# Mixer 1: three modulation units move from TensorE to VectorE, and the places at which units are loaded and finished move

## What is computed

```python
c_act = jax.nn.silu(c)                                  # (1, 2048)
mod = (c_act @ w_ada[l] + b_ada[l])[:, None, :]         # w_ada is 2048 x 12288
sh1, sc1, g1, sh2, sc2, g2 = jnp.split(mod, 6, axis=-1)
h = rms_norm(x, norm_mix[l]) * (1.0 + sc1) + sh1
x = x + g1 * hybrid_mixer(h, w_in[l], w_out[l], ...)
...
proj = h @ w_in                                         # all heads from one projection
ret_out = retention_chunkwise(rq, rk, rv) ...           # 4 heads
rwkv_out = rwkv7_time_mix(...)                          # 8 heads, low-rank codes, a scan
moba_out = moba_attention(mq, mk, mv)                   # 8 heads, softmax
return jnp.concatenate([ret_out, rwkv_out, moba_out], axis=-1) @ w_out
```

## Time and profile before

| | us |
|---|---|
| median of 3 runs | 2505.76 |
| lowest, highest | 2505.07, 2507.09 |
| the profiled execution, its own time | 2505.68 |
| its span, first to last instruction | 2503.9 |
| PE busy | 2454.4 (98%) |
| DVE busy | 1543.8 (62%) |
| POOL busy | 1234.3 (49%) |
| ACT busy | 1130.6 (45%) |
| mean granted TensorE clock | 0.992 |

### The profile page before, as it was taken

How to read it: one execution, slowest core, us unless ns; L and a number is a source line. 1 busy time by engine, 2 the same in 40 slices (tenths; PEclk the granted TensorE clock), 3 DMA queues, 4 the chain that set the end, 5 groups by cost and what they waited for, 6 DMA issues and landing times.

```text
span 2503.9 us, 49446 instructions
## 1 busy us (share of the span) xinstructions
PE 2454.4 (98%) x19158; PEld 2258.4 (90%) x19158; DVE 1543.8 (62%) x2630; ACT 1130.6 (45%) x1351; POOL 1234.3 (49%) x502
## 2 busy tenths in 40 slices
PE   6999999999999999999999989999999999999998
PEld 5797998999999999998887968899999999998886
DVE  3537667666767777776666787366756756443333
ACT  2253334534444444454545444444444444454544
POOL 2674445775444444444444756575444444444443
PEclk9999999999999999999999989999999999999999
DMA  9974565796777777777776656476565575556553
GB/s 393 396 270 180 201 226 224 262 360 235 280 275 276 266 268 283 260 266 269 281 263 243 238 187 242 171 293 251 219 243 216 216 260 184 181 179 199 192 192 127
DMA packets 140524, 611.63 MB, mean 244 GB/s; under 512 B 15600, under 2 KB 15984, under 8 KB 115824
## 3 DMA queue, kind: packets, MB, share of 16 engines
q1 hardware_dynamic: 140112, 609.09, 66.8%
q10 hardware_dynamic: 288, 0.79, 0.1%
HBM read 607.72 MB, written 2.10 MB: 244 GB/s over the span
## 4 chain that ended last, share of the span: by engine, by line
issue 68%; POOL 30%; POOLq 1%; DMA 1%; ACT 0%
POOL wlo L1816 30%; DMA raw<-wstream 1%; POOLq L1813 1%; POOLq L1815 0%; POOLq L396 0%; ACT whi L1832 0%; POOL xT L1823 0%; POOLq L1816 0%; ACT hi_h L1832 0%; POOLq L3009 0%
## 5 line engine op out<-in xcount | busy, mean ns | idle before, releaser
L1816 POOL TENSOR_TENSOR wlo<-raw,whi 128x1024 fp32r<-128x1024 f32 x496 | 1230.6, 2486 | 1247.1 <-ACT whi L1832 1246.4
L1832 ACT ACTIVATE whi<-raw 128x1024 fp32r<-128x1024 f32 x760 | 800.8, 1059 | 923.9 <-PE psum L2059 775.1
L2059 PE MATMUL psum<-hi_h,whi 128*128 128x256 f32 x4224 | 1207.6, 286 | 5.5 <-DVE lo_h L2483 3.4
L2059 PE MATMUL psum<-hi_h,wlo 128*128 128x256 f32 x4224 | 1191.1, 282 | 0.0
L2059 PE MATMUL psum<-lo_h,whi 128*128 128x256 f32 x4224 | 1190.7, 282 | 0.0
L2059 PEld LDWEIGHTS psum<-hi_h,whi 128*128 128x128 f32 x4224 | 799.4, 189 | 19.6 <-issue 8.1
L2059 PEld LDWEIGHTS psum<-hi_h,wlo 128*128 128x128 f32 x4224 | 799.6, 189 | 1.5 <-issue 1.2
L2059 PEld LDWEIGHTS psum<-lo_h,whi 128*128 128x128 f32 x4224 | 799.2, 189 | 0.0
L2483 DVE TENSOR_TENSOR wlo<-raw,whi 128x1024 fp32r<-128x1024 f32 x264 | 388.1, 1474 | 280.2 <-ACT whi L1832 280.2
L2491 DVE SCALAR_TENSOR_TENSOR psum<-ada_raw,cact,psum 128x256 f32<-128x256 f32 x996 | 431.6, 485 | 28.3 <-DMA ada_raw<-adastream 18.1
L2059 PE MATMUL psum<-whi,gshi 128*128 128x512 f32 x704 | 276.4, 393 | 0.3 <-DVE wlo L2483 0.3
(11 more groups left out here) (175 smaller groups left out, 1585.1 us busy)
## 6 DMA issues: line engine op xcount, KB each, us to landing
raw<-wstream SPq DMA_DIRECT2D x760, 512.0 KB, 4.4
ada_raw<-adastream SPq DMA_DIRECT2D x168, 1024.0 KB, 6.7
arena<-adastream SPq DMA_DIRECT2D x24, 1024.0 KB, 18.1
xT<-x_in SPq DMA_DIRECT2D x8, 512.0 KB, 7.2
gs_pages<-tabs_in SPq DMA_DIRECT2D x2, 512.0 KB, 4.3
gs_pages<-rw_in SPq DMA_DIRECT2D x2, 512.0 KB, 7.0
y_out<-xT SPq DMA_DIRECT2D x2, 512.0 KB, 3.2
y_out<-xT ACTq DMA_DIRECT2D x1, 512.0 KB, 2.7
```

Source lines behind the costliest of these rows:

```text
L1816: nc.gpsimd.tensor_tensor(wlo[:, q, :], raw[:, q, :], whi[:, q, :].bitcast(F32), ALU.subtract).then_inc(sem.lo_ready, 1)
L1832: return nc.scalar.activation(out_, in_, ACT.Copy, scale=scale)
L2059: return nc.tensor.matmul(o, lhsT, rhs, start=start, stop=stop, skip_group_check=True)
```

## The change

- Units 16, 17 and 29 are made by DVE; only 18 and 28 remain with PE. `LATE_UNITS1` starts one unit earlier.
- DVE makes units 16 and 17 ahead of the token shift of the fourth group, and units 29 to 32 at the stage's end, with the second attention round between the 7th and 8th product of unit 31.
- PE finishes unit 16 after slab 28, inside `G_LORA`; unit 29 after slab 91; unit 30 after slab 95; unit 31 after slab 100. The spots at slabs 36, 88 and before `moba_scores(1)` are gone.
- SP's loads move: unit 17's from slabs 36 and 37 to 32 and 34, unit 30's from 88 and 89 to 94 and 96, unit 31's from 96 and 97 to 98 and 100, unit 32's from 100 and 101 to 103, both.

```diff
-SPOTS1 = (32, 36, 40, 44, 48, 52, 56, 60, 64, 68, 72, 76, 80, 84, 92, 96, 104)
+SPOTS1 = (28, 36, 40, 44, 48, 52, 56, 60, 64, 68, 72, 76, 80, 90, 94, 99, 104)
...
-LATE_UNITS1 = (START_UNITS + 14, MIX_UNITS1[1])
+LATE_UNITS1 = (START_UNITS + 13, MIX_UNITS1[1])
...
 def by_pe(u):
-    return u < LOOP_UNITS[0] or LOOP_UNITS[1] <= u < LATE_UNITS1[0]
+    return u < START_UNITS or u == LOOP_UNITS[0] - 1 or LOOP_UNITS[1] <= u < LATE_UNITS1[0]
...
-        first = spots[u - units[0] - 1] + 4 if u > units[0] else spot - 6
+        first = spots[u - units[0] - 1] + 4 if u > units[0] else spot - 2
...
-        gap = 2 if late else 3 if u == LOOP_UNITS[1] else 1
+        gap = 2 if late or u in (START_UNITS + 1, LATE_UNITS1[0] + 1, LATE_UNITS1[0] + 2) else 3 if u == LOOP_UNITS[1] else 1
+        gap = 0 if u == MIX_UNITS1[1] - 1 else gap
...
             group(G_LORA, 0, 4)
-            group(G_LORA, 4, 8)
+            group(G_LORA, 4, 5)
             spot()
+            group(G_LORA, 5, 8)
...
             group(G_TQK, 2, 4)
-            spot()
             pe.wait_ge(sem.lora_out, 1)
...
             moba_values(0)
-            fill(4)
+            fill(12)
             spot()
+
             fill(8)
             spot()
-
-            fill(10)
+            fill(2)
+            moba_scores(1)
+            fill(8)
             spot()
-            moba_scores(1)
-            fill(10)
+            fill(2)
             moba_turn(1)
...
                 if e == 3:
-                    unit_rows()
+                    loop_products(-3, 0, 16)
+                    loop_products(-2, 0, 16)
                 dve.wait_ge(sem.rw_self, e + 1)
...
+            loop_products(10, 0, 16)
             loop_products(11, 0, 16)
-            loop_products(12, 0, 16)
+            loop_products(12, 0, 7)
             dve.wait_ge(sem.mo_out, 1)
             moba_bias(1)
-            loop_products(13, 0, 10)
+            loop_products(12, 7, 16)
             moba_norm(1)
-            loop_products(13, 10, 16)
+            loop_products(13, 0, 16)
```

More of the change, by code:

```diff
@@ L2461, in _ @@
                 slab(n, pair_of(g), hhi[:, 2 * i:2 * i + 2, :], hlo[:, 2 * i:2 * i + 2, :], i == 0, i == GS - 1)
-            st.update(unit=MIX_UNITS1[0], units=MIX_UNITS1, spots=SPOTS1, slabs=3 * GS, after_taken={MIX_UNITS1[0]: 8})
+            st.update(unit=MIX_UNITS1[0] + 1, units=MIX_UNITS1, spots=SPOTS1, slabs=3 * GS, after_taken={})
             pe_mix1(pe, st, mm, part, spot)
```

## The result

| | before | with the change |
|---|---|---|
| median of 17 runs each, us | 2505.07 | 2510.21 |
| lowest, highest | 2503.11, 2507.09 | 2507.20, 2512.97 |
| the profiled execution, its own time | 2505.68 | 2507.36 |
| its span | 2503.9 | 2505.5 |
| mean granted clock of that execution | 0.992 | 0.991 |

The ratio is 1.0019, 95% interval 1.0013 to 1.0026: slower by 3.3 to 6.5 us. The forecast was 2501.6, between 2499.6 and 2504.3. The profiled execution with the change is one of the fastest of its 17, and is 1.68 us above the one before. So about a third of the loss can be read from the two traces; the rest has to come from the comparisons of runs.

The account below looks back on a forecast made before the run. PE, busy 98% of the span, was taken as the bound. From the profiled 2505.68 us, 3.8 in the low-rank chain and 0.3 at the stage's end were subtracted, giving 2501.6 us, range 2499.6 to 2504.3.

Parts of the forecast that it names:

- What goes from PE: Units 16, 17 and 29 leave PE's list: 2.03, 1.83 and 1.83 us, together 5.69; finishing of units costs the same.
- The units' cover at the fourth group: Units 16 and 17 fit into DVE's 21.38 us wait before the fourth group's token shift and cost nothing.
- the signs listed as wrong: DVE waiting for `ada_raw` in unit 17, no wait before the shift, `wlo` above 2.5 us, or no gap in `moba_turn(1)`.
- ACT and DVE have to be free for it; DVE was idle for some us ahead of each of its steps there: Low-rank chain: its steps follow PE's second product, 3.86 us earlier, so the scan begins 3.8 us earlier.
- the low-rank chain keeps one unit's gain: Rival: ACT's or DVE's work sets the chain, so 3.8 us becomes about 2.0; 2503.4 us, chance 0.13.
- What runs beside POOL: DVE's unit products beside POOL's `wlo` (2.40 us, under a slab's 2.88 on PE) would cost POOL nothing that shows.
- The stage's end, the wait: `moba_turn(1)`: slab 103 queues behind unit 32's load, PE waits 1.3 us, and 0.3 us of unit 29's gain is left.
- load plus slab: 6.1 us: Stage's end: slab 103, issued at 479.6 behind unit 32's load, lands 6.1 us after that load's issue, at 485.4.
- SP's wait starves the ring: Rival: unit 32's second half delays slabs 103 to 107; with unit 31's loads late, near 2511 us; chance 0.06.

Follow-up runs that it names:

- e5: e3 with ACT's rounding of slabs 40 to 42 made later, and POOL's `wlo` of them with it; 2500.05 us, ratio 0.9977 to the kernel before.
- e8: e1 with ACT's rounding of slabs 40 to 42 made later; 2500.44 us, ratio 0.9980 to the kernel before.
- e9: e3 with only POOL waiting: its `wlo` of slab 40 held until DVE's column work is done; 2501.79 us, ratio 0.9982 to the kernel before.
- e7: The kernel before with only ACT's rounding of slabs 40 to 42 made later, no unit moved; 2504.61 us, ratio 0.9994 to the kernel before.
- e2: The kernel before with only the change's late part (unit 29 by DVE, the stage's end and its loads); 2506.09 us, ratio 1.0004.
- e4: The kernel before with SP holding slab 103 until the second round's exponentials are made, no unit moved; 2507.91 us, ratio 1.0013.
- e1: The change without its late part: only units 16 and 17 moved to DVE; 2504.51 us, ratio 0.9999 to the kernel before.
- e3: The change with the load of unit 32's second half ahead of slab 105 instead of 103; 2505.03 us, ratio 0.9998 to the kernel before.
- e6: The change with only ACT's rounding of slabs 40 to 42 made later, unit 32's loads as in the change; 2505.45 us, ratio 0.9999 to the kernel before.

## Why the prediction was wrong

**What goes from PE: right.** 96 records, three units; finishing costs what it did.

**The units' cover at the fourth group: right.** Unit 16 ran 144.24 to 152.65 (forecast 143.96 to 152.4), unit 17 155.88 to 164.30 (155.5 to 163.9), the shift began at 166.14 (165.8) behind a wait of 1.85 (1.9). The second low-rank product came at 177.59 (near 177.2). None of the signs listed as wrong showed there: POOL's `wlo` beside the products took 2.40.

**"ACT and DVE have to be free for it; DVE was idle for some us ahead of each of its steps there": this step failed.** The transposes ahead of the scan began 0.96 us earlier, not 3.8 (1.3, if the 0.35 by which this execution was behind at 142 is added). DVE had one idle time of 3.02 us in the chain's second half, ahead of 184.73, and three steps behind it with no idle at all. I moved the chain by 3.8 us as a block and did not ask what stands beside it. POOL does not move with DVE: it follows ACT's `whi`. Where before the two TENSOR_TENSOR fell into a gap of POOL's, they now fell on two `wlo` and cost 4.2 us more; the scan cost 2.1 more, the steps with `mu` 2.0 more, and the last column steps, which had met POOL before, 4.4 less. That is 3.9 us more; less the row copy that is gone (0.41) and 0.23 at the first step, 3.3. DVE's steps began 1.24 us earlier (173.63 against 174.87), the 3.02 of idle went into them, and 0.96 was left at their end. e5, e8 and e9 take away the collisions behind 187, and PE's early stretch is 4.9 to 5.5 us shorter than before. That holds the column steps' old collision too; against e7, which is before without it, e8 is 3.9 us shorter (62.40 to 58.48), the gain of the two units in full.

The rival with this place, "the low-rank chain keeps one unit's gain", had the right engine ("ACT's or DVE's work") and came nearer (2.0 us kept; 1.0 to 1.3 were), but had no reason for it that names POOL. Its price of 2503.4 still counted a gain at the stage's end.

**What runs beside POOL: tried on the wrong instructions.** The rows: TENSOR_TENSOR on two operands in SBUF, 1.24 us each alone (2.48 for two) and 3.34 beside a `wlo`; four TENSOR_SCALAR in SBUF 1.14 alone, 5.50 beside; the products, whose second large operand is in PSUM, 0.53 a piece beside POOL, and POOL 2.40 beside them. The Trainium skill says in "SBUF — State Buffer", "Who interferes with whom", that a VectorE instruction with two SBUF inputs contends with a GpSimd instruction that reads SBUF, and that `tensor_scalar` can do so in its two-port modes. The trace agrees with the first by 3.34 against 1.24; the TENSOR_SCALAR here contended too, at 5.50 against 1.14, and whether they ran in such a mode no run shows. The prediction quoted the first half, tried it on the unit products, found nothing, and left the chain's own TENSOR_TENSOR out. Its "blocks" is one side only: the scan and the `wlo` each took longer where they came second, as the last section has it.

**The stage's end, the wait: mechanism right, size wrong.** PE entered `moba_turn(1)` 1.46 us ahead of where the early part alone would have put it (forecast 1.63; `moba_turn(0)` waited 0.39 us for ACT where 0.2 was priced), and SP's list held slab 103 behind unit 32's second half. The term that was mis-sized is "load plus slab: 6.1 us", taken from one row of before. Here slab 103 could be rounded 7.1 us after the load's issue (478.77 to 485.86), in e2 6.2; the load was issued 0.5 us later than its forecast. The wait was 2.59 where 1.3 was expected, and in e2, 1.32.

**No term for the clock: this step was missing.** The sum had PE's waits at their length. In the profiled execution the late wait cost 1.3 us beyond it (15.31 less 11.41, less 2.59; 1.07 of it behind `moba_turn(1)`), in e4, where it stands alone, 1.6 (15.27 less 11.41, less 2.28). This, and the wait's 1.3 us over forecast, are most of why the stage's end lost 2.4 us where 0.3 was to be gained (0.96 ahead at the transposes, 1.48 behind at slab 104).

Sum in the profiled execution: forecast -4.08 against its own time, measured +1.68. Of the 5.76 between them the chain has 2.8, PE's stay in `moba_turn(1)` 1.6 (4.26 us where 2.7 was forecast, 1.3 of it the longer wait), the clock behind it 1.1; 0.3 is left.

**What stays open.** The median is 3 us further up than the profiled execution shows. Over the 17 runs with the change the mean granted clock averages 0.9900, over the runs of before 0.9915 to 0.9918, and the runs at 0.989 took 2511.3 to 2513.0, those at 0.991 and 0.992 2507.2 to 2508.9. So the other executions lost more clock than the profiled one; where, no trace shows. The place ahead of the bonus sums is likely, as the change has a wait of 2.82 us there, and e1 and e3, with the same wait, had the low clock behind it. The means over the runs point the same way: 0.9911 with the early wait alone (e3, its runs of before 0.9918), 0.9907 with the late one alone (e6, its runs of before 0.9915), 0.9900 with both. That is argued, not shown. Low clocks also come and go where nothing was edited (560 to 620 us: 0.97 before, 1.00 with the change, each in its profiled execution).

Why the two halves, at 0.9999 and 1.0004 alone, come to 1.0019 together is another matter. e3 has both parts and the early wait and stands at 0.9998, so what is lost in addition goes with the late load: in e2 its wait was 1.32 us and lengthened PE's stretch by 1.3, in the change 2.59 and by 3.9.

The rival "SP's wait starves the ring" had the right queue and the right side, with 9.6 us from unit 31's loads; those came in time, and unit 31 ended at 478.74, not near 489. That its price of 2511 lies so near the measured 2510.21 is luck. The sum needed 4.1 us more of delay to turn the sign, and they came from the low-rank chain and from the wait and clock at the stage's end.

## What to carry to other kernels

An engine's idle time covers added work only as long as the engines beside it are as they were. Before a chain is moved earlier, look at what each of its instructions will then run beside, POOL's with two operands in SBUF first. A wait of PE that is short on paper is priced with the clock behind it, and a load that waits for a result stands behind the slabs that don't. Two edits that each measure as nothing can be worth 0.2% together, if each lays bare the other's bound.

## What was not expected of the hardware

- Order decides who pays. The scan of the decays took 2.29 us when it began 0.04 us ahead of a `wlo`, and that `wlo` and the next together 7.73; begun behind a running `wlo`, it took 4.39.
- A column operand did not act as a second one: products with `ada_raw` in SBUF, a column and PSUM ran at 0.53 us beside POOL's 2.40.
- The granted clock fell behind PE waits of 2.28, 2.54 and 2.59 us at `moba_turn(1)` (0.57 to 0.65 in the four us around its end), not behind one of 1.32; behind the wait of 2.8 ahead of the bonus sums it fell in e1 and e3 (0.57 and 0.65) and stayed at 1.00 in the profiled execution of the change. The same wait can cost its length, or over 1 us more (early stretch 62.69 with the change, 63.83 in e1).
